# A two-model block on one core: token-major first feed-forward chunk, a rebuilt gated recurrence, a new order in the first blocks, and transposes of the identity during waits

## The chip, the cores and the metric

The kernel runs on one core of one Trainium2 chip. The metric is the device time of one execution in microseconds (us), lower is better. TensorE (PE) does matrix products, VectorE (DVE) and ScalarE (ACT) elementwise work, GpSimd (POOL) one kind of subtraction, and SyncE (SP) issues the weight transfers.

## What is computed

256 tokens of width 1024 pass through two models, one after the other. Everything is float32.

- First block, layer 0: RMS norm, one wide projection, attention over dilated windows in three groups of eight heads merged by softmax weights, cross attention to a memory of 256 rows, a gate silu(gate), an output projection and the residual.
- First block, layer 1: the same frame, with a gated linear recurrence (HGRN2) in place of the attention: `S_t = diag(f_t) S_{t-1} + k_t^T v_t ; o_t = q_t S_t`, eight heads of 128, then an RMS norm of o per head.
- Second block, four layers. Their mixers are gated linear attention (GLA, layers 0 and 3: four heads, keys 128 wide and values 256 wide, `scores = q.k.exp(-|L_t - L_s|)`), latent attention (MLA, layer 1) and a gated convolution (layer 2). After every mixer:

```python
x = layer_norm(ALPHA * x + h, ln_g[i, 0], ln_b[i, 0])
x = layer_norm(ALPHA * x + sq_relu_mlp(x, mlp_w1[i], mlp_w2[i]), ln_g[i, 1], ln_b[i, 1])
x = x + jax.nn.sigmoid(x @ ple_w_gate[i]) * (p[i] @ ple_w_proj[i])
```

The hidden width of the feed-forward part is 4096.

## The kernel before

**Units and splits.** All weights are laid out beforehand as units of 128 x 2048 floats (1 MB), in the order of use. SP loads unit n into a ring of four buffers (`raw`). Each product is made of three passes over values split in a high and a low part (`passes`, L935): ACT writes the high part `whi` (L1283, function `hi`), DVE or, in the feed-forward part, POOL writes the low part `wlo` (L1593 function `lo`, L903). `ahead(n)` stands in the queues of ACT and DVE at chosen places and means `hi(n + 3)` and `lo(n + 2)`.

**Steps.** `plan()` writes one list of steps by hand, and each engine runs through the same list in order, doing its own share of every step: `proj` (a unit of a projection into the banks `PP[0]`, `PP[1]`), `out` and `tail` (units of an output projection into the four banks `PQ`), `turn` (four 128 x 128 transposes on PE at L1111, then ACT writes the high part at L1406 and DVE the low part at L2079 of `XT` or `YT`), `post` (evacuation after a projection), `ahead`, and so on. A step that waits therefore holds back whatever is behind it on that engine.

**Forms of a product.** Token-major: the activations are the stationary operand, 512 output columns for each matmul, bank b holds tokens 128b to 128b+127, so bank 0 needs the first half of the tokens alone. Feature-major (`fm=True`): the weights are the stationary operand and 256 tokens stream, so every matmul needs both halves.

**Feed-forward.** Eight chunks of 512 hidden columns; a chunk is two units of `mlp_w1` (feature-major) and two of `mlp_w2`. DVE squares the relu (`hsq`, L2318), ACT and DVE split it into `YT`. Chunks 0 and 1 are peeled, the rest is a loop. The first unit of chunk 0 is issued after the layer norm of both halves has been transposed (`turn("x", 1, 0)`). After the last chunk comes a layer norm (L2265 to L2309) and the gate product `ple_w_gate` in steps `half` and `gate_quarters`, in between `turn` steps of the next input.

**Recurrence.** `levels()` runs nine steps for a half of the heads (HGRN, twice) or all heads (GLA, twice): for level l DVE makes distances of the next level (L1955, L1957, `distances`), ACT their exp (L1477), DVE the decayed q and k (L1931, L1933 for GLA, L1936, L1938 for HGRN), PE a small product, and DVE moves the wanted blocks of the result to `AT` (`evacuate`, L1975, L1977, L1984, L1987). Between levels stand the `cover` units, large projections for PE. `oscan` multiplies AT by v, and DVE norms the result (L2198 to L2218); `ymul` (L2155) then multiplies by the gate.

Of the kernel before, what the change touches and what calls it, by code (L numbers as in the profile page):

```python
# [24 lines left out]
P = 128  # L25
# [23 lines left out]
def plan():  # L49
# [62 lines left out]
    def unit(step, what, ahead=True, **f):  # L112

        units.append(what)
        m = len(units) - 1
        add(step, n=m, ahead=ahead and not hold[0], **f)
        if hold[0]:
            behind.append(lambda: add("ahead", n=m, on="sv"))
# [16 lines left out]
    def pieces(w, col, tag, src="X", feature_major=False, **f):  # L135
# [5 lines left out]
        def one(u, ahead=True, between=()):  # L141
            f = dict(g=g, u=u, src=src, fm=feature_major)
            unit("proj", (w, "P", u, col), ahead=ahead, banks=(0,) if between else (0, 1), **f)
            if between:
                while between:
                    between.pop(0)()
                add("proj", n=len(units) - 1, ahead=False, banks=(1,), **f)
# [15 lines left out]
    def project(w, col, tag, before_vector=None, between=None, **f):  # L163

        g, one, scalar_post, vector_post = pieces(w, col, tag, **f)
        one(0, between=late)
# [7 lines left out]
        one(1, ahead=tag not in ("qk", "fq"), between=[turn_first] if early else ())  # L174
# [4 lines left out]
        if tag in ("qk", "fq"):  # L179
            add("ahead", n=m, on="sv")  # L180

        after_unit()
        vector_post(fields)
# [14 lines left out]
    def turn(src, h, c, dst, k, pre="tsrc", late=False, a=0, later=0):  # L198

        add("turn", src=src, h=h, c=c, dst=dst, k=k, t=n["t"], ts=n["ts"], pre=pre, src_n=n["src"] + later, a=a,  # L200
# [10 lines left out]
    def begin_output(w, rows, src="Y"):  # L211
# [5 lines left out]
        def one(u, first=False, whole=False):  # L217
            unit("out", (w, "Q", u, 0), g=g, u=u, first=first, whole=whole, src=src, conv=conv, heads=len(heads))
# [16 lines left out]
    def output(w, src="Y", before_tail=None):  # L235
        g, one, tail = begin_output(w, 1024, src)
        one(0, first=True)
# [7 lines left out]
    def layer_norm(g, early):  # L245
# [8 lines left out]
        if not early:  # L254
            for c in range(2):
                quarter(1, c)
            for c in range(2):
                turn("x", 0, c, "X", 4 * c)
            return
        add("ln", g=g, h=1, part="sum", c=0)  # L260
        turn("x", 0, 0, "X", 0)
        add("ln", g=g, h=1, part="stat", c=0)
# [15 lines left out]
    turn("mg", 0, 1, "Y", 4)  # L278
    add("first_units", s=(0,), v=())
    turn("mg", 1, 0, "Y", 0)  # L280
    turn("mg", 1, 1, "Y", 4, late=True)
    add("first_units", s=(1, 2), v=(0, 1))
    add("squares", what="mem")
    vg = project(("w_mem_kv", 0), 512, "v", src="M", par=0,
# [10 lines left out]
    project(("w_in_a", 0), 9216, "qk", gain=6, rot=False, dst="q")  # L295
# [8 lines left out]
    for hq in range(2):  # L304
        for g in range(3):
            col = g * 1024 + hq * 512
            last = hq == 1 and g == 2
            vg = project(("w_in_a", 0), 6144 + col, "v", par=par, between=(lambda: merge(0, 0, 1)) if last else None)
            project(("w_in_a", 0), col, "qk", gain=g, rot=True, dst="q", between=(lambda: merge(0, 2)) if last else None)
            project(("w_in_a", 0), 3072 + col, "qk", gain=3 + g, rot=True, dst="k")  # L310
# [42 lines left out]
    def turn_tok(c):  # L353
# [3 lines left out]
    add("floors")  # L357
    project(("w_mem_kv", 1), 0, "qk", gain=1, rot=False, dst="k", between=lambda: turn_tok(0),
            before_vector=lambda: turn_tok(1))
    project(("w_in_b", 0), 3072, "qk", gain=0, rot=False, dst="q")  # L360
    quad("mem", vg, par=2, g=3)

    def levels(kind, hg, cover, pp=False):
# [4 lines left out]
        at = [int((i + 1) * every) for i in range(len(cover))]  # L368
# [10 lines left out]
        while cover:  # L379
# [11 lines left out]
            between=lambda: add("fgate", hg=0, part=0, gf=gf, heads=len(heads)))  # L391
    add("fgate", hg=0, part=1)
    drain()
    add("ymul", chunk=2, layer=1, second=0)
    n["vtok"], c1 = cover_of(wb, 2048 + 512, "vtok", c=1)
    c1[0]()
    for h in range(H2):
        turn("y", h, 2, "Y", 8)
    levels("hgrn", 0, c1[1:] + cover_of(wb, 3584, "gate", buf="y", gh=0)[1])
    add("ymul", chunk=0, layer=1, second=0)  # L400
# [6 lines left out]
    project(wb, 512, "fq", feature_major=True, scale=1.0, hg=1, second=0,  # L407
            between=lambda: (turn_y0(), add("fgate", hg=1, part=0, gf=gf, heads=len(heads))))
    add("fgate", hg=1, part=1)
    c1 = cover_of(wb, 3584 + 512, "gate", buf="y", gh=1)[1]  # L410
    c1[0]()
    c1[1]()
# [1961 lines left out]
```

## Time and profile before

| | |
|---|---|
| device time, three runs | 2029.96, 2027.54, 2028.56 us (median 2028.56) |
| the profiled execution | 2030.67 us, of it 2028.9 us span (first to last instruction) |
| busy | PE 1907.0, DVE 1206.5, ACT 910.5, POOL 593.2 us |
| granted TensorE clock, mean | 0.974 |

PE is busy 94% of the span. A busy microsecond says nothing of whether the engine ran at its full clock of 2.4 GHz or at the lower level of 1.2 GHz; the granted clock (1.00 is 2.4 GHz, 0.50 is 1.2 GHz) says that for a stretch.

### The profile page before, as it was taken

The page shows a single profiled execution, that of the slowest core. Times are in us where ns is not written, and L with a number is a line of the kernel's source. Part 1 is how long each engine was busy: PE and PEld are TensorE (multiplying, and loading weights), DVE is VectorE, ACT ScalarE, POOL GpSimd, SP SyncE. Part 2 cuts the span into 40 slices and gives each one's busy share as a digit, 9 for nine tenths or more (in the row PEclk, how much of TensorE's full clock was granted, in tenths as well). Part 3 has the DMA queues.
Part 4 walks back from the last instruction along what each step waited for, and adds up shares of the span by engine and source line. Part 5 has one row for each costly group of instructions (what it writes and reads, how often), then busy time and mean ns, then how long its engine had stood idle before and what let it go on. Part 6 is the DMA issues. An engine that isn't in the chain of part 4 may idle for free.

```text
span 2028.9 us, 27379 instructions
## 1 busy us (share of the span) xinstructions
PE 1907.0 (94%) x11072; PEld 1679.5 (83%) x11072; DVE 1206.5 (59%) x2062; ACT 910.5 (45%) x981; POOL 593.2 (29%) x132
## 2 busy tenths in 40 slices
PE   7999999998988988999999999999999988899998
PEld 6888888878877877999788899889899877779996
DVE  6787798867777687322767332566532466853226
ACT  5655555454353434444354444344444334334442
POOL 0000000000000003788101787400678600047870
PEclk9999999998999998999999999999999999989999
DMA  7434434542233325555433455445555532254551
GB/s 292 156 136 181 150 125 166 210 180 104 88 120 110 129 78 194 184 186 189 181 140 125 175 198 186 146 166 195 201 192 183 204 128 106 78 218 168 199 193 42
DMA packets 53556, 324.95 MB, mean 160 GB/s; under 512 B 8624, under 2 KB 12080, under 8 KB 16208
## 3 DMA queue, kind: packets, MB, share of 16 engines
q1 hardware_dynamic: 45200, 309.97, 41.8%
q10 hardware_dynamic: 8256, 13.58, 2.1%
q8 instruction: 70, 1.15, 0.2%
q14 instruction: 30, 0.25, 0.0%
HBM read 322.48 MB, written 1.05 MB: 159 GB/s over the span
## 4 chain that ended last, share of the span: by engine, by line
PE 73%; DVE 20%; ACT 3%; issue 3%; SPq 1%; DMA 0%; DVEq 0%; ACTq 0%
PE project L935 40%; PE output L935 26%; DVE wlo L1593 3%; PE turn L1111 1%; ACT whi L1283 1%; DVE XTl L2079 1%; DVE arena L1705 1%; DVE tok L2290 1%; PE output L1076 1%; SPq L866 1%; PE output L1053 1%; DVE arena L1931 1%; DVE arena L1933 1%; DVE arena L1957 1%; DVE st L2272 1%
## 5 line engine op out<-in xcount | busy, mean ns | idle before, releaser
L903 POOL TENSOR_TENSOR wlo<-raw,whi 128x2048 fp32r<-128x2048 f32 x128 | 593.0, 4661 | 1388.5 <-ACT whi L1283 1371.7
L1283 ACT ACTIVATE whi<-raw 128x2048 fp32r<-128x2048 f32 x291 | 554.7, 1914 | 474.3 <-PE project L935 310.0
L935 PE MATMUL project<-XTh,whi 128*128 128x256 f32 x1488 | 426.4, 287 | 4.1 <-DVE XTl L2079 3.1
L935 PE MATMUL project<-XTh,wlo 128*128 128x256 f32 x1488 | 424.4, 285 | 0.0
L935 PE MATMUL project<-XTl,whi 128*128 128x256 f32 x1488 | 424.2, 285 | 0.0
L2318 DVE TENSOR_TENSOR arena<-arena 128x512 f32<-128x512 f32 x64 | 142.8, 2265 | 462.0 <-ACT arena L1543 462.0
L1593 DVE TENSOR_TENSOR wlo<-raw,whi 128x2048 fp32r<-128x2048 f32 x163 | 376.9, 2322 | 38.8 <-ACT whi L1283 38.0
L935 PE MATMUL output<-whi,YTh 128*128 128x512 f32 x736 | 291.4, 396 | 11.4 <-DVE YTl L2079 11.4
L935 PEld LDWEIGHTS project<-XTh,whi 128*128 128x128 f32 x1488 | 289.3, 194 | 7.2 <-DVE XTl L2079 4.9
L935 PEld LDWEIGHTS project<-XTh,wlo 128*128 128x128 f32 x1488 | 289.1, 194 | 1.0
L935 PE MATMUL output<-wlo,YTh 128*128 128x512 f32 x736 | 289.2, 393 | 0.0
L935 PEld LDWEIGHTS project<-XTl,whi 128*128 128x128 f32 x1488 | 288.9, 194 | 0.0
L935 PE MATMUL output<-whi,YTl 128*128 128x512 f32 x736 | 288.9, 392 | 0.0
L935 PE MATMUL project<-whi,XTh 128*128 128x512 f32 x624 | 255.1, 409 | 8.9 <-DVE wlo L1593 4.5
L935 PE MATMUL project<-whi,XTl 128*128 128x512 f32 x624 | 245.4, 393 | 0.0
L935 PE MATMUL project<-wlo,XTh 128*128 128x512 f32 x624 | 244.9, 392 | 0.0
L935 PEld LDWEIGHTS output<-whi,YTh 128*128 128x128 f32 x736 | 140.2, 190 | 39.9 <-DVE YTl L2079 12.0
L935 PEld LDWEIGHTS output<-whi,YTl 128*128 128x128 f32 x736 | 139.7, 190 | 29.8
L935 PEld LDWEIGHTS output<-wlo,YTh 128*128 128x128 f32 x736 | 140.0, 190 | 27.6
L935 PEld LDWEIGHTS project<-whi,XTh 128*128 128x128 f32 x624 | 118.9, 191 | 37.1 <-DVE wlo L1593 8.5
L935 PEld LDWEIGHTS project<-whi,XTl 128*128 128x128 f32 x624 | 118.2, 189 | 26.0
L935 PEld LDWEIGHTS project<-wlo,XTh 128*128 128x128 f32 x624 | 118.7, 190 | 23.3
(245 smaller groups left out, 2113.0 us busy)
## 6 DMA issues: line engine op xcount, KB each, us to landing
raw<-in_units SPq DMA_DIRECT2D x291, 1024.0 KB, 4.8
arena<-in_ln_g ACTq DMA_DIRECT2D x8, 512.0 KB, 3.9
arena<-in_ln_b ACTq DMA_DIRECT2D x8, 512.0 KB, 4.9
arena<-in_mem_norm_gain ACTq DMA_DIRECT2D x2, 512.0 KB, 5.0
tok<-in_mem SPq DMA_DIRECT2D x2, 512.0 KB, 5.7
xres<-in_x SPq DMA_DIRECT2D x1, 1024.0 KB, 12.8
arena<-in_mem ACTq DMA_DIRECT2D x1, 1024.0 KB, 6.8
arena<-in_p ACTq DMA_DIRECT2D x4, 256.0 KB, 4.3
```

Of the source, the lines that this page charges most:

```text
L866: sp.dma_start(dst, src).then_inc(s, 16)
L903: pool.tensor_tensor(wlo[:, slot, :], raw[:, slot, :], whi[:, slot, :], ALU.subtract).then_inc(lo_pool, 1)
L935: mm = pe.matmul(out, x if x_stationary else w, w if x_stationary else x, start=start and i == 0, stop=stop and i == 2, skip_group_check=True)
L1053: mm = pe.matmul(PQ[h2][:, h * S:h * S + n], qkT[:, h2, h * P:(h + 1) * P], qkT[:, h2, S:S + n], start=True, stop=True)
L1076: mm = pe.matmul(PQ[3][:, h * P:(h + 1) * P], pT[:, h2, x * P:(x + 1) * P], v, start=kt == 0, stop=kt == len(mine) - 1)
L1111: mm = pe.transpose(PT[f["t"] % 2][:, x * P:(x + 1) * P], s, ident[:, :])
L1283: act.activation(whi[:, slot, :], raw[:, slot, :], ACT.Copy).then_inc(hi_done, 1)
L1593: dve.tensor_tensor(wlo[:, slot, :], raw[:, slot, :], whi[:, slot, :], ALU.subtract).then_inc(lo_dve, 1)
L1705: ins = dve.scalar_tensor_tensor(out=v, in0=v, scalar=st[:, 24 + x:25 + x], in1=gain, op0=ALU.mult, op1=ALU.mult)
L1931: dve.tensor_tensor(QE[l % 2], q, Dx, ALU.mult).then_inc(dve_own, 1)
L1933: dve.tensor_tensor(KE[l % 2], k, Dx, ALU.mult).then_inc(z_ready, 1)
L2318: dve.tensor_tensor(hsq[:, b, :], relu[:, b, :], relu[:, b, :], ALU.mult).then_inc(hsq_ready, 1)
```

## The change

- **First feed-forward chunk.** Chunk 0 of every layer is token-major and split by banks: both units on bank 0 (tokens 0 to 127) first, with the second half's `turn` steps between them and under a name of their own, "B", so that only bank 1 waits for them. ACT and DVE make relu and square by halves (`rows`), and `hsq` is turned back by two `turn("h", ...)` steps while chunk 1 runs. The peeled part and the counters shift by a chunk.
- **Recurrence.** For HGRN the levels 6, 7, 8 and for GLA the levels 0, 6, 7, 8 are evacuated by ACT (`scalar_evacuates`), in one to eight pieces; ACT also takes a copy of level 8's distances into its exp. GLA's two decay products become one instruction of 2048 columns. Level 0 of GLA waits no more for DVE; for HGRN a step `z0` does that earlier. `oscan` multiplies the gate by gain/2 while PE works, does one chain of 1/sqrt for both halves, and writes the gated result, so `ymul` after it goes. `ahead` and `ymul` steps move; covers of HGRN stand one level earlier. The output product of HGRN is cut so that `turn` steps stand inside its last quarter.
- **Gate product.** The last quarter (`GATE_ORDER[3]`) doesn't wait for the turns issued before it (`turned`), and `turn("x", 1, 1)` moves ahead of the last `half`.
- **First blocks.** Order of the first turns and `lo(0)`, token-major bank split in the first projection, `sines` apart from `init`, `merge` steps a projection later, the second unit of a memory projection no longer waits for turns (`turned=True`), the key's normalization moves behind a unit of the next projection (`vector_later`).
- **`busy` steps.** PE transposes the identity into a bank that is free: 12 times before the first projection, 11 times after the first `turn` of the layer norm that follows the feed-forward part, 12 times ahead of `turn("x", 1, 0)` there.

No transfer is added or taken away, and the order of the units is the same.

```diff
@@ plan(): feed-forward part
-        turn("x", 1, 0, "X", 0)
-        turn("x", 1, 1, "X", 4, late=True)
         n0, g = len(units), n["p"]
-        unit("proj", ("mlp1", i, 0, 0), g=g, u=0, src="X", fm=True, banks=(0, 1))
+        rows = dict(g=g, src="X", fm=False)
+        unit("proj", ("mlp1", i, 0, 0), u=0, banks=(0,), begin=True, **rows)
         flush()
+        turn("x", 1, 0, "X", 0, rows="B")
+        unit("proj", ("mlp1", i, 1, 0), u=1, banks=(0,), begin=False, ahead=False, **rows)
+        turn("x", 1, 1, "X", 4, rows="B", late=True)
+        normed = n["src"]
+        add("rows", g=g, h=0)
+        add("proj", n=n0, u=0, banks=(1,), begin=False, ahead=False, **rows)
+        add("proj", n=n0 + 1, u=1, banks=(1,), begin=True, ahead=True, **rows)
         add("loadln", i=i, k=1)
-        unit("proj", ("mlp1", i, 1, 0), g=g, u=1, src="X", fm=True, banks=(0, 1))
-        add("mlp", i=i, n=n0, g=g, q=n["q"], src_n=n["src"])
+        add("rows", g=g, h=1)
+        turn("h", 0, 0, "Y", 0)
+        unit("proj", ("mlp1", i, 0, 1), g=g + 1, u=0, src="X", fm=True, banks=(0, 1))
+        turn("h", 1, 0, "Y", 0, late=True)
+        unit("proj", ("mlp1", i, 1, 1), g=g + 1, u=1, src="X", fm=True, banks=(0, 1))
+        add("mlp", i=i, n=n0, g=g, q=n["q"], src_n=normed)
@@ gate product
         half((0, 0), (0, 1), (1, 0))
         gate_ahead(0, "s")
+        add("busy", bank="P", p=n["p"], turns=12)
         turn("x", 1, 0, "X", 0, late=True, later=1)
...
         turn("x", 0, 1, "X", 4, late=True)
+        turn("x", 1, 1, "X", 4, late=True)
         half((3, 0), (3, 1))
         gate_ahead(1, "sv")
-        turn("x", 1, 1, "X", 4, late=True)
@@ the level's evacuation, on ScalarE
+        def scalar_evacuates(g, l):
+            return l in ((0, 6, 7, 8) if g else (6, 7, 8))
...
                         ins.then_inc(e_ready, 1)
                         last.other(e_ready, nth("e"))
+                        evacuate(f, l - 1, f["L"] - 1)
@@ VectorE, level of GLA
-                    dve.tensor_tensor(QE[l % 2], q, Dx, ALU.mult).then_inc(dve_own, 1)
-                    last.own()
-                    dve.tensor_tensor(KE[l % 2], k, Dx, ALU.mult).then_inc(z_ready, 1)
+                    both = ar((0, 8)[l % 2], 2048).rearrange("p (a b) -> p a b", a=2)
+                    dve.tensor_tensor(both, ar(24, 2048).rearrange("p (a b) -> p a b", a=2),
+                                      Dx.unsqueeze(1).to_broadcast([P, 2, 1024]), ALU.mult).then_inc(z_ready, 1)
@@ TensorE
+                elif kind == "busy":
+                    if f["bank"] == "P":
+                        pe.wait_ge(p_evac[0], f["p"])
+                    bank = PP[0] if f["bank"] == "P" else PQ[0]
+                    for x in range(f["turns"]):
+                        pe.transpose(bank[:, (x % 4) * P:(x % 4 + 1) * P], ident[:, :], ident[:, :])
```

## Rows read from the trace of the kernel before

**Rows 1.** The page: busy time by engine, and its chain by engine.

```profile
PE 1907.0 (94%) x11072; PEld 1679.5 (83%) x11072; DVE 1206.5 (59%) x2062; ACT 910.5 (45%) x981; POOL 593.2 (29%) x132
...
PE 73%; DVE 20%; ACT 3%; issue 3%; SPq 1%; DMA 0%; DVEq 0%; ACTq 0%
```

**Rows 2.** The chain of waits, whole span: start us, us, what.

```profile
842.15 11.51 PE project L935 x96
853.67 10.91 PE output L935 x48
...
965.77 11.15 PE output L935 x49
...
1972.55 11.15 PE output L935 x49
```

**Rows 3.** Windows: length, busy us (instructions) by engine, PE clock, DMA share, GB/s.

```profile
800.80:806.20 5.40, 2.11 (x9) 1.57 (x9) 3.93 (x11) 3.52 (x4) 1.84 (x1) 0.74 0.53 194
```

**Rows 4.** The chain between ple projection and feed-forward, layer 0.

```profile
802.87 0.76 DVE xres L2309
...
803.67 1.13 PE turn L1111 x4
...
806.20 25.05 PE project L935 x192
```

**Rows 5.** The page's group of squares: count, busy us, mean ns, idle before.

```profile
L2318 DVE TENSOR_TENSOR arena<-arena 128x512 f32<-128x512 f32 x64 | 142.8, 2265 | 462.0 <-ACT arena L1543 462.0
```

**Rows 6.** The chain after the feed-forward part, layer 0.

```profile
996.20 0.66 PE turn L1111 x4
...
1006.68 8.46 PE output L935 x36
...
1018.56 4.52 PE output L935 x12
```

**Rows 7.** The same in layer 3.

```profile
2002.99 0.66 PE turn L1111 x4
```

**Rows 8.** Windows in which PE only transposes.

```profile
651.60:655.60 4.00, 1.78 (x14) 1.15 (x11) 2.42 (x5) 2.72 (x5) 0.00 (x0) 1.00 0.00 0
633.00:637.60 4.60, 1.26 (x8) 0.84 (x8) 4.60 (x6) 1.19 (x2) 0.00 (x0) 0.84 0.19 22
```

**Rows 9.** Timeline of ACT at the start: start, us, what, idle before.

```profile
28.83 1.92 ACT L1283 ACTIVATE whi<-raw 128x2048 fp32r<-128x2048 f32 x1 [1.90 <-DMA raw<-in_units]
```

**Rows 10.** The chain at the second memory projection.

```profile
409.36 5.71 PE project L935 x24
```

**Rows 11.** Windows over HGRN's two ladders and GLA's first.

```profile
497.20:538.00 40.80, 38.43 (x209) 34.09 (x209) 34.88 (x47) 15.93 (x15) 0.00 (x0) 0.83 0.27 102
583.60:623.50 39.90, 35.34 (x208) 31.54 (x208) 33.88 (x47) 13.89 (x11) 0.00 (x0) 0.91 0.30 110
699.30:748.30 49.00, 41.38 (x232) 36.36 (x232) 46.04 (x56) 17.85 (x16) 0.00 (x0) 0.93 0.34 126
```

**Rows 12.** DVE's groups by form in GLA's first ladder.

```profile
L1593 DVE TENSOR_TENSOR wlo<-raw,whi 128x2048 fp32r<-128x2048 f32 x5 | 11.4, 2275 | 0.0
L1987 DVE COPY_PREDICATED arena<-arena,output 128x512 f32<-128x512 uint8 x12 | 8.0, 721 | 0.1
L1933 DVE TENSOR_TENSOR arena<-arena 128x1024 f32<-128x1024 f32 x6 | 7.3, 1215 | 0.0
...
L1984 DVE TENSOR_TENSOR arena<-output,ident 128x512 f32<-128x512 f32 x2 | 1.3, 680 | 0.0
```

**Rows 13.** DVE's evacuations by form in HGRN's first ladder.

```profile
L1975 DVE COPY_PREDICATED arena<-arena,output 128x512 f32<-128x512 uint8 x7 | 6.2, 885 | 5.1 <-PE output L1161 5.1
```

**Rows 14.** The chain into and out of HGRN's first ladder.

```profile
492.17 1.29 DVE arena L2155 x2
...
501.06 3.68 PE output L1161 x16
...
537.98 2.08 PE output L1186 x8
```

**Rows 15.** The chain around HGRN's second ladder.

```profile
574.21 2.30 DVE wlo L1593
...
637.67 12.49 PE output L935 x43
```

**Rows 16.** The chain after GLA's first ladder.

```profile
762.97 4.40 DVE wlo L1593 x2
...
769.87 7.06 PE output L935 x24
```

More of the change, by code:

```diff
@@ L115, in unit @@
         m = len(units) - 1
-        add(step, n=m, ahead=ahead and not hold[0], **f)
+        add(step, n=m, ahead=False if hold[0] else ahead, **f)
         if hold[0]:
@@ L173, in project @@
             between()
-        one(1, ahead=tag not in ("qk", "fq"), between=[turn_first] if early else ())
+        one(1, ahead=tag not in ("qk", "fq", "f"), between=[turn_first] if early else (), turned=turned)
         fields = scalar_post()
@@ L236, in output @@
         g, one, tail = begin_output(w, 1024, src)
-        one(0, first=True)
+        one(0, first=True, scan=w[1] + 1 if w[0] == "gla_w_out" else 0)
         flush()
@@ L261, in layer_norm @@
         turn("x", 0, 0, "X", 0)
+        add("busy", bank="P", p=n["p"], turns=11)
         add("ln", g=g, h=1, part="stat", c=0)
@@ L277, in plan @@
     turn("mg", 0, 0, "Y", 0)
[L278 to L282, printed above, removed]
+    turn("mg", 0, 1, "Y", 4, late=True)
+    add("first_units", s=(0,), v=(0,))
+    turn("mg", 1, 0, "Y", 0, rows="B")
+    turn("mg", 1, 1, "Y", 4, rows="B", late=True)
+    add("first_units", s=(1, 2), v=(1,))
     add("squares", what="mem")
+    late.append(lambda: None)
+    add("busy", bank="Q", turns=12)
     vg = project(("w_mem_kv", 0), 512, "v", src="M", par=0,
@@ L367, in levels @@
         every = 9 / (len(cover) + 1)
-        at = [int((i + 1) * every) for i in range(len(cover))]
+        at = [int((i + 1) * every) - (kind == "hgrn") for i in range(len(cover))]
         gq = n["pd"]
@@ L439, in gla @@
         levels("gla", 0, cv + cg)
-        add("ymul", chunk=0, layer=0, second=1)
-        project(w, 2560, "gate", buf="G", gh=1)
-        for h in range(H2):
-            turn("y", h, 0, "Y", 0)
+        _, one, scalar_post, _ = pieces(w, 2560, "gate", buf="G", gh=1)
+        one(0)
+        one(1, ahead="s", between=[lambda h=h: turn("y", h, 0, "Y", 0) for h in range(H2)])
+        add("ahead", n=len(units) - 1, on="v")
+        scalar_post()
         add("ymul", chunk=1, layer=0, second=1)
@@ L1557, in ahead_at @@
                             hi(per8 * 8 + m, m % RING, per8 * 2 + (m // RING + 1))
-                    chunk(g0, 0, True)
-                    square(0, 0)
-                    for u in range(2):
-                        ahead(n0 + 2 + u)
-                    chunk(g0 + 1, 1)
+                    chunk(g0 + 1, 1, True)
                     square(1, 1)
```

316 lines of the change are left out of this document (210 added, 106 removed).

## Prediction

> **What bounds the kernel now.** First the page: PE is busy 1907 of 2028.9 us, and it is 73% of the chain that ended last, DVE 20% [rows 1]. So only three things can shorten the run: less work on PE, fewer waits of PE, or PE's clock higher. Then the chain over the whole span: a chunk of the feed-forward part is a steady pair of 11.51 us (96 matmuls of 256 columns, 0.120 us each) and 10.91 us (48 of 512 columns, 0.227 each) [rows 2], with nothing between them; there is nothing to win inside the loops. The waits lie where one product ends and the next needs the result turned and split: the entry to the feed-forward part, the gate product after it, the recurrences. In the window before the first feed-forward unit PE works 2.11 of 5.40 us and the clock is 0.74 [rows 3]. In the recurrences' ladders the windows show DVE busy 34.88 of 40.80 and 33.88 of 39.90 us (HGRN) and 46.04 of 49.00 us (GLA), clock 0.83 to 0.93 [rows 11]: there DVE sets the pace, PE only shares it.
>
> The profiled execution took 2030.67 us, 2.1 above the median of the runs, 2028.56. I make the sum against the first and take 2.1 off at the end. What a measurement of this kernel can tell from no change is about 0.2%, 4 us.
>
> **Feed-forward entry, four times.** Before, PE has finished the ple projection at 800.8 and issues the first unit at 806.20, since both halves of the norm must be turned; chunks 0 and 1 then take 25.05 us, to 831.25 [rows 3, 4]. That is 2.0 us over two times 11.51, a clock of 0.5 at its start. Now bank 0 can go at 800.8, because the first half was turned earlier. Twelve matmuls of 512 columns: 10.91/4 = 2.73 us, to 803.5. The turn of the second half still waits for DVE (its source, 802.87 plus 0.76) and starts at 803.67 [rows 4], four transposes of 0.11 (0.44). Twelve more, to 806.9, a turn, 24 for bank 1, 5.46, to 812.8; turn of h, feature-major unit 5.75, turn of h, 5.75: 825.3. Gain 6.0 us: PE no longer idles, 0.6 less for the token-major form, 0.9 more for two added turns. What is late next? h's first half is relu at 807.5, square behind it. A square takes 2.27 us where POOL works beside it instead of the 0.7 of its neighbours [rows 5, 12]; even held back by a whole POOL subtraction (593.2 us over 128 of them [rows 1], 4.6 each) it ends by 812.8, and the second half by 818 against a need at 819. From both sides: 4 (each square late by 1 us) to 6.5. Take 6.0, times four, **24.0**.
>
> **Gate product.** After the last chunk the next turn is `turn("x", 1, 0)`. In layer 0 the clock was 0.5 for part of the way, in layer 3 it wasn't; from the last piece of the loop to this turn it is 996.20 - 965.77 = 30.43 us there and 2002.99 - 1972.55 = 30.44 here [rows 2, 6, 7]. So the layer norm on DVE ends this stretch, and what `busy` saves in it is nothing: 12 transposes (1.3 us) go where PE would wait about 1.9. Next, `gate_quarters` starts at 1006.68 behind the split of the last turn; moved forward, that split is ready, but `lo` of the fourth unit now comes after it on DVE and ends near 1006.2: 0.5, times four, 2.0 (0 to 1.9 each). Then the last quarter: its three neighbours take 8.46 us (36 matmuls) and end at 1014.9; two turns, 16.0; then PE waits for a split that this quarter doesn't read, to 1018.56, and 12 matmuls take 4.52 us instead of 2.73, the clock having dropped [rows 6]. Without the wait: 2.56 + 1.79 = 4.3, times three (the last layer has no such turns), 12.9. DVE's work for the next layer's turn hangs on this quarter itself, so it moves along. **14.9** together, 11 to 18.
>
> **Ladders.** A ladder is as long as DVE's list. GLA: taken off DVE are level 0's two products (1.36), of the 12 predicated copies two (1.44), levels 7 and 8 (1.4), level 8's copy of distances (0.4), and half a us of overhead where two 1.215 us products become one; one `lo` (2.27) goes into an earlier wait of DVE [rows 12]. Added: a memset, some 0.4. That is 7.0; but behind level 6 stands a PE cover, so that PE (four covers of 5.7 and nine levels, some 38 us) takes over near the end: 6.4. After it: one chain of 1/sqrt instead of two, `ymul` (1.29) gone, and of the two `lo`'s (4.40) that stood before the output product only one is left ahead of it: by DVE's list the split of y is ready 17.1 us after `oscan` begins, before it was 21.5 (748.33 to 769.87); then 24 matmuls at full clock instead of 7.06 us, 1.6 [rows 16]. 12.4 for each GLA.
> HGRN 1: `ymul` (1.29), a `lo` (2.2) and two splits stood before level 0; PE's first product of level 1 ran at 501.06 [rows 14]. Now `ymul` is done earlier, DVE gives `z0` where `ymul` stood, at 492.2, and has distances (1.3), the two splits (1.3), one `lo` (2.3), distances (1.3) and the decayed q and k (1.3) ahead of level 1: 499.7, with one cover (5.5) already done by PE. DVE's list behind it loses 2.6 us, and of its 5.1 us of waits for PE [rows 13] most. The end comes at about 530.3 instead of 537.98, and `oscan` (24 small products, 5.5 us at half clock) takes 2.7 [rows 14]. With a wait of 1.3 gone after it: 11.8. HGRN 2: the unit behind 574.21's `lo` [rows 15] starts at once, level 0 two us earlier, level 1 by four, 9 us at `oscan`; then 0.6 before the tail at 637.67, which still waits for a `lo`, and 2.7 of waits for residual turns that now stand inside the last quarter: 12.3.
> That makes 49. What ACT's pieces cost is in no row: the nearest are whole-bank copies of 0.6, so level 6 of GLA in eight pieces is 1 to 5 us of ACT's time, behind it the exp of level 8. From below the four ladders keep only their earlier starts and the part behind them, 28; from above 52. I take 22 for each kind, **44**.
>
> **First blocks.** `turned=True`: unit 1 started at 409.36 [rows 10] behind a split it doesn't read, now at 407.8: 1.5. `vector_later` frees a unit by 1.7, but the next turn needs the same DVE list's end: 0. Sine and `hi` order 1.0, `merge` moved to where DVE has room 1.0. **3.5**, 0 to 5.5.
>
> **Start.** `lo(0)` moves ahead, so the first product starts 1.8 us earlier, and `busy` may raise the clock before it. Both end in a wait: ACT's `hi` of unit 4 waits for the transfer until 28.83 and lasts 1.92 [rows 9], the evacuation of the first projection stands behind it on ACT, and the second projection behind that. SP issues that transfer behind the constants, untouched. **0**, from -2 (PE idles 5 us now, the clock may fall) to 3.
>
> **What `busy` is worth.** PE does nothing but transposes for 4.0 us in one window and the clock stays 1.00; with 8 in 4.6 us it is 0.84 [rows 8]. So transposes hold the clock if there are enough, and they cost nothing where PE waits anyway. The Trainium skill ("TensorE: Matmul & The Clock Gate", Part 4, PE-mode transpose) says against this that transposes don't count as the array being busy. By that rule the `busy` steps would only be in the way: the first rival below; by the row they are free. The window with 14 transposes speaks against the page.
>
> **Sum.** 24.0 + 14.9 + 44 + 3.5 + 0 = 86.4. 2030.7 - 86.4 = 1944.3; less 2.1: **1942** us.
>
> **Rivals.**
> - The clock falls in spite of the transposes. The two `busy` steps after each layer norm then run at half clock, 23 transposes of 0.22 instead of 0.11, and stand past the time PE has (1.9 and 1.4 us): about 3 us a layer, and the last quarter at half clock again, 1.8: 15 to 19 us, **1959**. Against it [rows 8]. 0.06.
> - ACT takes over the ladders. For it: eight pieces in front of level 8's exp, all in order on one queue. Then only 15 of 44 come, **1971**. Against it: ACT is busy 18 us of 49. 0.18.
> - Everything listed comes, PE runs through the ladders at full clock, and the start helps by 3: 105, **1923**. 0.12.
> - Slower: ACT's moved evacuations hold PE at every level. There are 14 of them (3, 3, 4, 4), and 86 us are to be eaten, so it decides from 6.2 us each; a piece would have to cost ten times a whole-bank copy. **2035**. 0.03.
> - Nothing changes: the entry and the ladders wait for something else that the chain hides (a transfer). The same place would have to be bound twice in all four layers. **2028**. 0.02.
> - The forecast: 0.59; its own range 1931 to 1955.
>
> Range 1925 to 1970: it takes in the forecast, the first rival, half of ACT's and half of the full gain. Faster 0.95, same 0.02, slower 0.03.
>
> **What would show it.** The first feed-forward unit right behind the ple projection and chunks 0 and 1 over 24.5 us after it; no wait ahead of the last gate quarter and 2.7 us for it; ladders of about 43 us (GLA) and 33 (HGRN) with DVE still the fuller engine; the second projection still at 31.4. Wrong it would be if DVE waits for ACT in the ladders, if the turn of h waits for a square, or if the clock is lower after a `busy` step than without.

## The result, and the profile after

The changed kernel takes **1970.98 us**, median of 4 runs (1968.69 to 1971.86); the kernel before took 2029.26 beside it (2027.54 to 2030.31). The ratio is 0.9712, 95% interval 0.9695 to 0.9729: 58 us faster, where I had forecast 87 and a time of 1942. The profiled execution took 1971.44 us, 59.2 less than that of before.

The page of the kernel after, busy time and chain by engine, against [rows 1]:

```profile
PE 1893.4 (96%) x11016; PEld 1664.1 (84%) x11016; DVE 1185.0 (60%) x2006; ACT 921.3 (47%) x1021; POOL 596.5 (30%) x132
...
PE 78%; DVE 16%; ACT 3%; issue 2%; SPq 1%; DMA 0%; ACTq 0%; DVEq 0%
```

PE's busy time hardly moved (13.6 us less); its share of the chain grew from 73 to 78%, DVE's fell from 20 to 16%. So waits for DVE did go. The chain of the kernel after at the entry to the feed-forward part, layer 0, against [rows 3, 4]:

```profile
788.28 5.48 PE project L977 x24
793.76 0.64 PE turn L1155 x4
794.40 2.76 PE project L977 x12
797.16 0.44 PE turn L1155 x4
797.60 5.49 PE project L977 x24
...
803.53 5.75 PE project L977 x48
...
809.71 5.76 PE project L977 x48
815.47 10.91 PE output L977 x48
```

The first unit follows the ple projection at once, every step has the length that was forecast, and no wait is left; the two turns of h wait for no square. The chain of the kernel after around the gate product, same layer, against [rows 6]:

```profile
972.30 0.67 PE turn L1155 x4
...
990.25 8.41 PE output L977 x36
998.67 0.87 PE turn L1155 x8
999.54 2.74 PE output L977 x12
```

The last quarter stands right behind two turns and takes 2.74 us, before it waited and took 4.52.

The windows of the kernel after, from a ladder's first product to `oscan`: HGRN's two, then GLA's two; then two stretches at the start. Columns as in [rows 3], against [rows 11]:

```profile
496.94:541.50 44.56, 38.07 (x208) 34.08 (x208) 37.10 (x48) 18.08 (x20) 0.00 (x0) 0.84 0.31 117
583.12:622.07 38.95, 36.33 (x208) 32.39 (x209) 33.22 (x42) 14.85 (x15) 0.00 (x0) 0.88 0.32 119
697.00:744.25 47.25, 39.74 (x233) 34.90 (x233) 41.66 (x42) 23.63 (x32) 0.00 (x0) 0.96 0.31 112
1663.25:1707.99 44.74, 38.08 (x232) 33.47 (x232) 40.39 (x40) 23.69 (x32) 0.00 (x0) 1.00 0.33 117
26.30:31.70 5.40, 1.22 (x8) 0.80 (x8) 3.91 (x4) 3.23 (x5) 0.00 (x0) 0.75 1.02 416
31.76:39.39 7.63, 7.63 (x26) 6.13 (x27) 5.35 (x15) 3.21 (x4) 0.00 (x0) 0.73 0.40 164
```

Here most of the missing time lies. HGRN's first ladder is not shorter than before but 3.8 us longer (44.56 against 40.8), with DVE busy for 37.10 us of it and the clock at 0.84. Part of that is only where the window begins. Counted from the same `hi` on ACT, first in the kernel before, then after,

```profile
484.48 1.93 ACT whi L1283
```

```profile
488.96 1.92 ACT whi L1344
```

PE comes to level 0 at 8.0 instead of 12.7 us and to `oscan` at 52.5 instead of 53.5: a start 4.7 us earlier, and only 1.0 of it left at the end, where 7.7 were forecast (530.3 instead of 537.98). As a sign I had named ladders of about 33 us (HGRN) and 43 (GLA), though my own times for HGRN's first, 492.2 to 530.3, make 38.1; they took 44.6, 39.0, 47.3 and 44.7. The chain of the kernel after through it shows where, against [rows 14]:

```profile
509.88 3.31 PE output L1221 x16
513.19 7.44 PE project L977 x24
...
524.15 5.54 PE project L977 x24
529.69 1.75 PE output L1221 x16
...
535.33 3.68 PE output L1221 x16
...
541.50 2.07 PE output L1246 x8
```

The same 16 products take 1.75 us at one place and 3.31 and 3.68 at two others, the same unit 5.54 and 7.44.

Setting the start of every weight unit on PE in one trace against the other (how much later or earlier it comes, from one end of a stretch to the other) gives where the 59.2 us came from, beside the terms of the prediction:

| stretch | forecast | traces |
|---|---|---|
| feed-forward entry, 4 times | 24.0 | 23.5 |
| gate product, 4 times | 14.9 | 15.3 |
| HGRN, both ladders and what follows each | 22 | 6.7 |
| GLA, both | 22 | 18.3 |
| first blocks | 3.5 | -2.3 |
| start | 0 | -2.2 |

Nearly all that is missing is in three terms: HGRN 15, first blocks 6, GLA 4; the start's loss lies on my lower bound.

### The profile page after: what moved, and what is told of

The parts are those of the page before. It is cut to its first block, busy times and chain, and to the rows that moved or that the text cites. A ratio compares the mean times of both kernels' runs of the same rounds, so it can differ in the third digit from the quotient of the medians.

```text
span 1969.6 us, 27242 instructions
## 1 busy us (share of the span) xinstructions
PE 1893.4 (96%) x11016; PEld 1664.1 (84%) x11016; DVE 1185.0 (60%) x2006; ACT 921.3 (47%) x1021; POOL 596.5 (30%) x132
## 4 chain that ended last, share of the span: by engine, by line
PE 78%; DVE 16%; ACT 3%; issue 2%; SPq 1%; DMA 0%; ACTq 0%; DVEq 0%
PE project L977 43%; PE output L977 26%; DVE wlo L1696 3%; PE turn L1155 2%; DVE arena L2036 1%; DVE arena L1808 1%; PE output L1118 1%; SPq L908 1%; ACT whi L1344 1%; PE output L1095 1%; PE output L1221 1%; PE turn L1074 1%; DVE arena L2059 1%; DVE st L1799 1%; DVE tok L2416 1%
## 5 line engine op out<-in xcount | busy, mean ns | idle before, releaser
L977 PE MATMUL project<-XTh,whi 128*128 128x256 f32 x1360 | 386.5, 284 | 0.0
L977 PE MATMUL project<-XTl,whi 128*128 128x256 f32 x1360 | 384.8, 283 | 0.0
L977 PE MATMUL project<-XTh,wlo 128*128 128x256 f32 x1360 | 384.8, 283 | 0.0
L977 PE MATMUL project<-whi,XTh 128*128 128x512 f32 x688 | 281.1, 409 | 7.1 <-ACT arena L1353 4.5
L977 PE MATMUL project<-whi,XTl 128*128 128x512 f32 x688 | 271.0, 394 | 0.0
L977 PE MATMUL project<-wlo,XTh 128*128 128x512 f32 x688 | 270.3, 393 | 0.0
L977 PEld LDWEIGHTS project<-XTh,whi 128*128 128x128 f32 x1360 | 260.8, 192 | 1.5 <-DVE XTl L2182 0.5
L977 PEld LDWEIGHTS project<-XTh,wlo 128*128 128x128 f32 x1360 | 260.9, 192 | 1.0
L977 PEld LDWEIGHTS project<-XTl,whi 128*128 128x128 f32 x1360 | 260.8, 192 | 0.0
L977 PEld LDWEIGHTS output<-whi,YTh 128*128 128x128 f32 x736 | 139.4, 189 | 31.7 <-issue 3.9
L977 PEld LDWEIGHTS project<-whi,XTl 128*128 128x128 f32 x688 | 130.5, 190 | 28.8
```

What stands on the lines that cost most here:

```text
L977: mm = pe.matmul(out, x if x_stationary else w, w if x_stationary else x, start=start and i == 0, stop=stop and i == 2, skip_group_check=True)
```

## The experiments

Theory 1: TensorE's clock. The change makes PE wait in new places and leaves small products between, the clock goes to 0.5 there, and PE takes over from DVE as what sets the ladders. Theory 2: ScalarE took over (the 0.18 rival). Theory 3: DVE's list is as long as ever and the moved parts are worth nothing. The first four kernels were compared on one chip, as were the next four, the four after them and the last three; between two chips the ratio to the kernel before is what counts, and its interval is 3 to 4 us to each side. Unless said otherwise a kernel is the changed one with the edit shown, and times are medians.

**Covers one level later again (e1).**

```diff
-        at = [int((i + 1) * every) - (kind == "hgrn") for i in range(len(cover))]
+        at = [int((i + 1) * every) for i in range(len(cover))]
```

> The changed kernel with one line undone: in the two HGRN ladders each covering projection goes behind the level at which it stood before, not one level earlier. Theory 1 (what was forecast for the HGRN ladders, some 24 us, was lost because moving the covers one level earlier puts a `lo` of 2.3 us in front of level 2's decayed q and k, and leaves PE with little but 64-column products at levels 7, 8 and in the output product, where its clock is at 0.5): the ladders from level 1 to `oscan`, now 37.2 us in the first, come down to 33 to 35, and the run takes 1963 to 1968 us instead of 1971. Rival 2 (the place of the covers is indifferent, since each costs the same 5.5 us of PE and 2.3 of DVE wherever it stands): 1970 to 1972. Rival 3 (the move is a gain that another loss hides): 1974 to 1978.

Measured: 1976.04 us (1975.22 to 1978.24), ratio 0.974 [0.9725, 0.9754]. 5 us slower: rival 3. In the trace 3.6 of them are in the two HGRN ladders. Moving the covers was a gain; my suspicion that the move itself had cost the time was wrong.

**Transposes in the waits of the HGRN ladders (e2).** A new kind of `busy` step writes into the bank of the next turn, which is idle there; besides those in the list below there are 4 ahead of each `oscan`, 57 in all:

```diff
+                    elif f["bank"] == "T":
+                        wait_bank(f["t"])
...
+            turns = {("hgrn", False): {2: 24, 7: 13}, ("hgrn", True): {2: 6, 7: 6}}.get((kind, pp), {}).get(l, 0)
+            if turns:
+                add("busy", bank="T", t=n["t"], turns=turns)
             add("lev", kind=kind, hg=hg, l=l, L=L + l, heads=len(heads), gq=gq, pp=pp)
```

> The changed kernel with transposes of the identity, into the bank of the next turn, in waits of the two HGRN ladders: 24 ahead of level 2's product in the first ladder (PE waits 3.7 us there), 13 ahead of level 7's, 6 ahead of levels 2 and 7 in the second, 4 ahead of each output product. Theory 1 (TensorE's clock, 0.84 and 0.88 over the two ladders, sets part of their length): the clock comes to 0.95 or more in both, level 2's product takes 1.9 instead of 3.3 us, level 7's 1.9 instead of 3.7, the unit behind level 2 5.5 instead of 7.4; the list of VectorE takes over sooner than all of it is won, so 3 to 5 us for each ladder, 1961 to 1966 us in all. Rival 2 (VectorE's list and ScalarE's queue set the ladders, a slow PE is hidden): 1970 to 1972, with the clock up. Rival 3 (transposes do not hold the clock here): the clock stays under 0.9 and the run takes 1971 to 1975, since transposes at half clock stand past the waits.

Measured: **1957.52 us** (1956.75 to 1961.05), ratio 0.9644 [0.963, 0.9659]: 13.5 us faster than the changed kernel, more than theory 1 asked for. The same two windows of this kernel:

```profile
499.14:538.38 39.24, 37.04 (x249) 33.25 (x249) 37.03 (x48) 18.08 (x20) 0.00 (x0) 1.00 0.36 131
578.59:614.57 35.98, 34.47 (x224) 30.58 (x225) 33.14 (x42) 14.86 (x15) 0.00 (x0) 1.00 0.37 128
```

DVE does the same work in both kernels (37.10 and 37.03 us, 48 instructions), ACT too; only PE was given 41 instructions more, and the window is 5.3 us shorter, at a clock of 1.00 instead of 0.84. DVE is now busy for 37.03 of 39.24 us: this is the ladder paced by DVE of which the prediction spoke, and it lasts about what was forecast (492.2 to 530.3, 38.1 us). By unit starts the stretch of both ladders is 13 us shorter than in the changed kernel. The Trainium skill ("TensorE: Matmul & The Clock Gate", Part 4, PE-mode transpose) says of transposes that the full clock "doesn't engage" for them. By that rule these two windows would have kept their 0.84 and 0.88; the runs contradict it.

**Transposes in the GLA layers alone (e3).** 12 ahead of `vtok`, 14 ahead of level 6.

> The changed kernel with transposes of the identity in two waits of each GLA layer: 12 between the gate's small product and the token-major projection (the clock falls to 0.5 for 3.4 us there in both layers), and 14 ahead of level 6's product (where it falls in the first layer only). Theory 1 (the clock): the two-unit projection ahead of the first ladder takes 11.2 instead of 12.8 us in each layer, and the first layer's cover behind level 6 5.5 instead of 6.6; both are on the chain that sets the end, so 2 x 1.6 + 0.9 = 4 us, 1967 us. Rival (the ladder's start waits for VectorE's or ScalarE's work of the same stretch anyway): 1970 to 1971.

Measured: 1973.37 us (1970.16 to 1973.95), ratio 0.9718 [0.9704, 0.9733]. No gain. In the trace the fall near 685 us is gone and another stands at 709.4 to 716.2; over both GLA stretches together the clock is about what it was, 0.95 and 0.98 (in the changed kernel 0.96 and 0.98). So this says only that curing one thin place of several needn't help.

**Start and sines (e4).**

```diff
     turn_tok_half(0)
+    add("busy", bank="Q", turns=28)
     add("scales", what="x")
...
-                elif kind == "sines":
+                elif kind == "sines_read":
                     dve.wait_ge(a2v, nth("a2v"))
```

`sines_read` is placed behind the next projection's scalar part.

> The changed kernel with two edits in the first 65 us: 28 transposes of the identity while PE waits for the second projection's first unit (26.3 to 31.8 us), and VectorE's wait for the sine table moved one projection later, to where its result is first needed. Theory 1: the unit at 31.8 us takes 5.5 instead of 7.6 us at full clock, 2.1 us; VectorE no longer idles from 56.5 to 59.5, which takes away the 2.5 us in which PE waits for a `lo` at 59.2 to 61.8. Together 4 to 4.6 us, 1966.5 to 1967 us. Rival (both gains end in the next wait for a transfer or for VectorE's list of the rotation at 64 to 67 us): 1969 to 1971.

Measured: 1965.85 us (1964.79 to 1971.57), ratio 0.9689 [0.9675, 0.9702]. The chain of this kernel at the start:

```profile
31.66 5.69 PE project L979 x24
37.35 0.88 PE turn L1157 x8
38.23 24.74 PE project L979 x108
```

The unit takes 5.69 instead of 7.63 us and PE runs on without a gap through the place where it waited for a `lo`; at the first turn of the merge, 331 us, this kernel is 4.6 us ahead. Its profiled execution is the slowest of its five: there the clock falls near 430 us, where it does not in the changed kernel (1.6 us lost), it is at 0.5 for 20.4 us of the first HGRN ladder (17.0 in the changed kernel; 1.5 lost) and for longer in the second, and the whole 4.6 us are gone at 600 us. The other four are 2.7 to 6.8 us faster. How the time follows the clock, by execution:

```
changed kernel   1968.69 us at 0.989   1970.52 at 0.987   1971.44 at 0.986   1971.86 at 0.987
e4               1964.79 us at 0.990   1965.54 at 0.987   1965.85 at 0.989   1968.85 at 0.986   1971.57 at 0.985
e2               1956.75 us at 0.995   1956.90 at 0.995   1958.15 at 0.995   1961.05 at 0.993
```

**Everywhere (e5).** e2 and e4 together, and 12 transposes ahead of `vtok`, 8, 12 and 12 ahead of levels 2, 4 and 6 in the GLA layers.

> The changed kernel with both earlier edits that made it faster (transposes of the identity in the waits of the HGRN ladders, 1957.5 us; transposes ahead of the second projection and VectorE's wait for the sines one projection later, 1965.9 us), and besides transposes in the waits of the GLA ladders: 12 ahead of the token-major projection, 8 ahead of level 2, 12 each ahead of levels 4 and 6. If the two gains are of separate places they add up: 1971 - 13.5 - 5 = 1952.5 us, and the GLA turns, which alone gave nothing, 0 to 4 more once the clock doesn't fall elsewhere: 1948 to 1953 us, clock 0.995 or more. If the start's gain ends in the ladders, as it did in the profiled run of that kernel (4.6 us at 331 us, 0 at 632 us), because the clock fell there, it should now last. If only the number of transposes in a stretch decided and the fall merely moves to the next thin place: 1956 to 1960 us, clock 0.99.

Measured: 1957.96 us (1954.74 to 1958.47), ratio 0.9648 [0.9635, 0.9662]. By the ratio no better than e2: the gains did not add. The profiled run is 6.9 us ahead of e2's at 338 us, but only 3.4 behind the first GLA ladder. In between its clock falls near 430 us, behind the delayed norm of the key (1.3 us lost), and at 622 us for 6.8 us, where PE waits ahead of the residual product (1.4).

**No transposes at all (e6).** The three `busy` steps of the change removed.

> The changed kernel without any of its transposes of the identity (12 at the start, 11 and 12 around the norm of each layer). My prediction held that they cost nothing and hold the clock in the gate stretch. By the clock theory the clock falls again near the norm in at least two of four layers, for 3 to 7 us each, and the units behind run at half speed for that time: 4 to 10 us more, 1975 to 1981 us. Rival (a transpose does not count for the clock, or the stretch ends with VectorE's norm anyway, as it did in before in layer 0 with a low clock and in layer 3 with a full one): 1968 to 1972 us.

Measured: 1969.94 us (1968.74 to 1974.11), ratio 0.9721 [0.9706, 0.9736]: the same time as with them. The clock does fall without them, in all four layers, at the end of the feed-forward part. First one of the four windows of this kernel, then the chain behind it:

```profile
970.00:973.40 3.40, 3.40 (x8) 2.75 (x9) 3.26 (x8) 1.91 (x1) 0.00 (x0) 0.50 0.00 0
```

```profile
975.20 0.76 DVE xres L2432
976.01 0.66 PE turn L1152 x4
```

The 8 products of the first gate quarter in this window run at half clock, 0.43 us from one to the next. But the turn behind them waits for the norm's second half on DVE (975.20 plus 0.76), as it does with the transposes, so a slow clock ahead of it costs nothing.

**Evacuations back on DVE (e7).** `scalar_evacuates` returns False; level 8 is a copy on DVE again.

> The changed kernel with all evacuations of the ladders' levels back on VectorE (three per HGRN ladder, four per GLA layer; level 0 by the product with the identity, level 6 of GLA by two masked copies); ScalarE keeps only the exps. Theory 1 (the loss is the clock): VectorE's list grows by 2.1 us in each HGRN ladder and 4 us in each GLA one, of which its waits for PE take up a part: 1974 to 1981 us. Rival 2 (ScalarE took over the ladders, the case that I gave 0.18 in my prediction): the evacuations and exps no longer queue on ScalarE and the run is faster than the changed kernel, 1960 to 1967 us.

Measured: 1971.05 us (1969.17 to 1977.89), ratio 0.9716 [0.9701, 0.9731]: the same by the medians, with a scatter of 8.7 us. Neither theory had this. The windows of this kernel, HGRN's two ladders, then GLA's:

```profile
500.32:542.30 41.98, 37.03 (x208) 33.26 (x208) 37.79 (x50) 16.14 (x16) 0.00 (x0) 0.87 0.33 122
585.47:626.06 40.59, 37.89 (x209) 33.80 (x209) 33.87 (x44) 12.91 (x11) 0.00 (x0) 0.84 0.31 115
701.02:748.97 47.95, 40.61 (x232) 35.94 (x232) 45.62 (x49) 18.89 (x18) 0.00 (x0) 0.93 0.31 110
1668.02:1714.42 46.40, 39.68 (x232) 34.86 (x232) 44.54 (x48) 18.98 (x18) 0.00 (x0) 0.96 0.31 112
```

Theory 2 falls: without any evacuation on ACT HGRN's two ladders are together 0.9 us shorter (82.6 against 83.5), GLA's two 2.4 us longer. The second number is what the moved evacuations were worth, where I had 8.4 for GLA; the medians cannot show it.

**The last quarter waits again (e8).** `turned=False` for it.

> The changed kernel with the last quarter of each gate product waiting again for the split of the last turn, which it does not read (three layers have turns there). The prediction took 4.3 us in each of three layers for this wait: 1.8 us of low clock behind it and 2.5 us of waiting. If that is right the run takes 1980 to 1984 us. Rival (the wait is mostly covered, since the next layer's first turn hangs on the same VectorE list): 1972 to 1976 us.

Measured: 1981.44 us (1979.62 to 1982.23), ratio 0.9772 [0.9757, 0.9787]. 10.5 us slower, somewhat less than the 12.9 of the prediction. The chain of this kernel there:

```profile
985.72 8.43 PE output L977 x36
...
996.23 1.21 DVE XTl L2182 x2
997.43 0.14 issue
997.57 4.34 PE output L977 x12
```

The wait and the slow quarter (4.34 us) are both back. In this trace that costs 4.2 us here and 4.4 in layer 2, but only 2.8 in layer 1, where the clock stays up and the quarter takes 3.01: that is why it is less than three times 4.3.

**Two more places (e9).** e5 with 30 transposes ahead of the residual product's third unit and 26 ahead of level 2 of the first GLA layer.

> The kernel with transposes everywhere (1958.0 us) with two more places: 30 ahead of the residual product's third unit, where PE waits from 619.1 to 622.8 us and then runs 36 matmuls for 11.3 us with the clock at 0.5 from 622.1 to 628.9, and 26 instead of 8 ahead of level 2 in the first GLA layer, where the clock falls at 693.8. Theory 1 (each fall of the clock that stands on the chain costs about half its length): 3.4 us and 1 to 1.7 us, 1953 to 1954 us. Rival (these stretches end with VectorE's work, and a full clock only lengthens the waits): 1957 to 1958 us.

Measured: 1955.27 us (1954.18 to 1955.62), ratio 0.9639 [0.9619, 0.9659]. First the chain of e5, then that of e9:

```profile
620.46 2.21 DVE wlo L1706
...
622.81 11.29 PE output L985 x36
```

```profile
619.69 3.50 PE turn L1178 x30
623.18 8.28 PE output L986 x36
```

30 were a few too many (the unit begins 0.2 us late by the rest of the trace), and it still wins: 36 products take 8.28 instead of 11.29 us. The trace puts 2.8 us on this place. The medians differ by 2.7, but the ranges overlap by 0.9 and the intervals of the ratios too, so the trace is the evidence. The second place gave nothing: the fall of the clock at 693.8 us is gone, and e9 is 2.6 us ahead before the ladder and behind it.

**First blocks undone (e10).** e5 with the merges and `vector_later` as before the change.

> The kernel with transposes everywhere (1958.0 us) with two edits of the first blocks undone: the merges of the dilated heads one projection earlier, as before, and VectorE's part of the memory key's norm directly behind its projection, not one projection later. The prediction put 1.0 us on the moved merges and nothing on the delayed norm; from the milestones of the two traces I read since that they lost 1.3 and 1.0 us. If that reading is right, undoing them gives 1955 to 1956.5 us; if the prediction was right, it costs 1 us, 1959 us; if the lost time at those places came with the clock at the start (28 transposes, now cured), 1958 us.

Measured: 1953.81 us (1953.41 to 1954.09), ratio 0.9634 [0.9614, 0.9654], outside the range of e5, though the intervals of the two ratios overlap. In the trace e10 is 1.2 us ahead of e5 at 330 us, where the merges stand, and 3.7 at 481 us, behind the delayed norm. So both moves cost time. Of the second's 2.5 us 1.3 came with the fall of the clock near 430 us, which e10 does not have.

**Evacuations on DVE, clock held (e11).** e7's edit in e5.

> The kernel with transposes everywhere (1958.0 us) with all evacuations of the ladders' levels back on VectorE. Without the transposes this same edit changed nothing (1971.1 against 1971.0 us). Theory 1, in its present form (VectorE's list sets a ladder's length only while TensorE's clock is held; where it falls, PE does, and a shorter list on VectorE gives nothing): with the clock held the edit costs what the prediction computed from VectorE's list, 2.1 us in each HGRN ladder and up to 4 in each GLA one, less its waits: 1963 to 1970 us. Rival (the moved evacuations are worth nothing in either case, since the way over ScalarE takes as long): 1957 to 1960 us.

Measured: 1960.06 us (1957.91 to 1961.2), ratio 0.9661 [0.964, 0.9682]: 2 to 3 us slower than e5, between the two theories, nearer the rival. The windows of GLA's two ladders, of e11 and then of e5 (HGRN's are 39.36 and 35.46 us in e11, 39.25 and 35.99 in e5):

```profile
682.27:730.33 48.06, 42.99 (x265) 38.42 (x265) 46.16 (x50) 18.77 (x18) 0.00 (x0) 0.96 0.30 110
1651.34:1697.72 46.38, 41.58 (x264) 36.82 (x264) 44.70 (x48) 19.00 (x18) 0.00 (x0) 1.00 0.32 113
```

```profile
681.59:728.86 47.27, 42.75 (x265) 38.20 (x265) 43.14 (x43) 23.50 (x32) 0.00 (x0) 0.96 0.31 112
1649.88:1694.75 44.87, 41.58 (x265) 36.83 (x265) 40.97 (x41) 23.64 (x32) 0.00 (x0) 1.00 0.34 118
```

DVE does 3.0 and 3.7 us more in GLA, the ladder is 0.8 and 1.5 longer. In HGRN DVE's busy time differs by only 0.7 us and the two ladders together are 0.4 shorter. These are the same amounts as in e7 (0.7 and 1.7), where the clock was not held, so my theory that a held clock would bring out the list's full price is wrong as well. Theory 3 is nearly right about this part.

**The kernel before, with transposes (e12).** 20 ahead of the turns at 492.9 us, 14, 10, 22 and 8 ahead of levels, 20 ahead of the residual product's third unit.

> The kernel before, with transposes of the identity in the waits of PE in and around its two HGRN ladders (20 ahead of the turns at 492.9 us, 14 and 10 ahead of level 0, 22 ahead of level 1 of the second, 8 ahead of level 8 of the first, 20 ahead of the residual product's third unit). The clock is at 0.5 for 17.1 + 6.8 + 6.8 + 6.9 us there. Theory A (the clock is a loss of its own, there before the change as well): half of most of it comes back, 8 to 14 us, 2015 to 2021 us. Theory B (before, VectorE's longer list set the ladders, and a slow PE was hidden under it; only the change made the clock the bound): 0 to 4 us, 2025 to 2029 us.

Measured: 2022.73 us (2020.88 to 2029.35, 10 runs), ratio 0.9975 [0.9963, 0.9988]: 6 us by the medians, between A and B. The windows of this kernel from the first product of each HGRN ladder to `oscan`:

```profile
499.67:534.87 35.20, 33.24 (x218) 29.80 (x217) 32.70 (x44) 15.10 (x15) 0.00 (x0) 0.99 0.25 95
578.35:615.10 36.75, 34.94 (x231) 31.35 (x231) 33.61 (x45) 13.90 (x11) 0.00 (x0) 1.00 0.31 113
```

40.8 us became 35.2 (39.5 became 36.8). The first number flatters: by unit starts PE is through the first `oscan` 5.6 us earlier than in the kernel before, and only 6.0 ahead where the residual product, which waits for DVE, goes on behind the second (631.7 instead of 637.7 us). So the clock was a loss before the change too; the changed kernel lost twice that. It did not do so by running at half clock for longer. The whole stretch from the `hi` above to the residual product, in the kernel before and in the changed one:

```profile
484.00:650.00 166.00, 144.70 (x820) 127.90 (x821) 127.81 (x192) 66.62 (x62) 0.00 (x0) 0.89 0.30 110
```

```profile
488.00:650.00 162.00, 144.42 (x826) 128.84 (x825) 120.09 (x181) 71.41 (x75) 0.00 (x0) 0.88 0.30 106
```

A mean of 0.89 over 166 us and one of 0.88 over 162 are both some 37 to 39 us at 0.5. Theory 1's first half, that the change makes the clock fall more, is not borne out; what changed is how much of a slow PE lies on the chain, now that DVE has 7.7 us less to do.

**All together (e13), without the norm's transposes (e14), with the covers later (e15).** e13 is e9 with e10's edits, and 12, 8 and 5 transposes ahead of level 0 of the HGRN ladders and of the gate's small product in GLA. e14 and e15 are without these three; e14 is besides without the 11 and 12 transposes around each norm, e15 has e1's line.

> All that helped, in one kernel: transposes in every wait found so far (those ahead of the residual product's third unit too), VectorE's wait for the sines later, the merges and the memory key's norm where they were before; and transposes in three more places where the clock still falls: 12 and 8 ahead of level 0 of the two HGRN ladders, 5 ahead of the gate's small product in the GLA layers. If the gains add, 1953.8 - 2.7 = 1951 us without the three new places, and with them 1949 to 1951 us. If the falls only move on: 1952 to 1954 us.

> The same as the last one without its three new places and without the 11 and 12 transposes around each layer norm (which the change brought, and whose absence cost nothing in the changed kernel: 1969.9 against 1971.0 us). If a held clock matters in the gate stretch only when nothing else hides it, as in the ladders, it shows now: four falls of 3.4 us, some 1.5 us over the four layers as in the trace of that kernel: 1952 to 1953 us. If the stretch always ends with VectorE's norm: 1951 us. If the transposes around the norm are what the gate product's gain hangs on: 1956 us or more.

> The same base (1951 us expected) with the covers of the two HGRN ladders one level later again. With the clock falling this cost 5 us (1976.0 against 1971.0). If the earlier place gains by VectorE's list (level 1 starts behind fewer of its operations) and the clock has no part in it: 4 to 6 us again, 1955 to 1957 us. If it gained only through where the clock fell: 0 to 2 us, 1951 to 1953 us.

Measured: e13 1953.85 us (1953.49 to 1954.6), ratio 0.9633 [0.9617, 0.965]. **e14 1951.37 us** (1950.18 to 1952.18), ratio 0.9621 [0.9605, 0.9637]. e15 1965.43 us (1963.17 to 1966.3), ratio 0.9688 [0.9672, 0.9704].

e13 has the highest mean clock of all, 0.998, and is not the fastest. The chain of e13 ahead of the first ladder shows why:

```profile
491.22 0.61 DVE YTl L2194
...
491.87 1.69 PE turn L1179 x12
493.56 2.56 PE output L1239 x12
```

The 12 transposes want the bank of the next turn, and here that bank is still being split by DVE. They wait until 491.87 us and level 0 waits behind them: 3.1 us late at `oscan` against e10. e14 lets the clock fall near every norm (mean 0.995) and is the fastest kernel of this study, 19.6 us below the changed one by the medians. e15 is 14 us slower than e14, more than either reading had, and no clean answer: with the covers later, the 24 transposes stand where PE does not wait (2.8 us in its way), and the clock falls elsewhere, 0.86 over the ladder. Whether the covers' place is worth its 5 us by DVE's order alone stays open.

## Why the prediction was wrong, step by step

- **Feed-forward entry**, 24.0: right, 23.5 in the traces, each sub-step within 0.1 us.
- **Gate product**, 14.9: right, 15.3; e8 gives 10.5 for the quarter alone where I had 12.9. The claim that the `busy` steps save nothing in this stretch held (e6): without them the clock falls, and nothing is lost. My first rival, that it falls in spite of them and costs 15 to 19 us, did not come: the last quarter takes 2.74 us.
- **HGRN ladders**, 22: this step failed, by 15 us. It read "A ladder is as long as DVE's list" and had `oscan`, 5.5 us at half clock, take 2.7. The second takes a full clock for granted, the first holds only under it. The clock of 0.83 and 0.91 [rows 11] and the slow products [rows 14] were there; I read these as the past and put no term on them for the future. The chain of the changed kernel shows PE, not DVE, at levels 2, 7, 8 and in `oscan`, which took 4.3. With the clock held and nothing else changed (e2) two ladders and what follows gave 13 us more, and the run 13.5. Of this about 6 could have been had before the change (e12). The rest, about 7, I read as hidden before under DVE's longer list, since the half-clock time was as long then; that is a difference of two experiments, and no run isolates it. Some 2 of the 15 us are not accounted for by it.
- **GLA**, 22: 18.3 came, 7.7 in the first layer and 10.5 in the second. The part behind `oscan` was right (17.25 us to the output product against 17.1). The evacuations were mis-sized: by DVE's list I had 4.2 us a ladder for what moved to ACT, e11 shows 0.8 and 1.5, e7 0.7 and 1.7, and for HGRN neither shows any. The clock is not the cause here: e13, at full clock through both GLA layers, passes the first only 0.6 us faster than the changed kernel. In the changed kernel's chain an ACT `hi` of 1.91 us (683.89) stands ahead of the gate's exponents, which it did not before; I did not test that.
- **First blocks**, 3.5: wrong in sign. `turned=True` gave 1.6 where 1.5 was forecast. The merges cost 1.2 instead of giving 1.0 (e10), `vector_later` cost between 1.0 (the two traces) and 2.5 us (e10, a fall of the clock at 427 us included) instead of nothing, and the DVE wait for the sine table cost 1.6 where I had a gain of 1.0; e4 took it away.
- **Start**, 0 with a bound of -2: -2.2, and by the mechanism named for that bound: PE idles from 26.3 to 31.7 us and the next unit takes 7.63 us. In e4 it takes 5.69, and its trace is 2.0 us ahead there.
- **Rivals.** 1971 us is the number I gave for ScalarE taking over, and it is the right number for a wrong reason: e7 takes that work off ScalarE and gets the same time. The rival that was missing is "the clock stays low in the ladders, where no transposes were put, and DVE no longer hides it". I had asked about the clock only where the change had `busy` steps.

Between e14 (77 us faster than before) and the 87 forecast lie GLA's 4, what is left of the first blocks, and gaps that I did not follow further.

## What to carry to other kernels

A slow PE can hide under the engine that paces a stretch. Shortening that engine's work uncovers it: before counting the gain, ask what PE does in each wait, and price the products behind it at the clock that the trace shows there. Fillers are worth having only where PE's products behind them are on the chain, and only into a bank that is free at that moment: 57 transposes in two ladders gave 13.5 us, 104 around the norms and at the start gave nothing, 12 into a bank still being read cost 3. A higher mean clock is not a shorter run.

## What the runs showed of the hardware

- Transposes of a 128x128 fp32 identity held the clock: in the ladders 0.84 became 1.00 with nothing else added. They took some 0.12 us each (30 in 3.50 us).
- Products of 64 columns in short bursts did not hold it: before level 2 of the second HGRN ladder PE waits about 1 us between two bursts of 16, and the clock is at 0.5 from 595.6 us.
- A program on one core, run again and again on one chip, varied by up to 8.7 us (e7; e4 by 6.8), and the slower executions mostly have the lower mean clock; comparisons of a few us need all executions, and a single trace can be the slowest.
